# Two expert routers fed from the raw residual by halves, and expert weights requested before the routers run

## The reference, cut to what matters

```
h      = rmsnorm(x, g) * (1 + scale) + shift        # g, scale, shift: 1024 long
logits = h @ w_router + b_router                    # block 1: 32 experts, the 4 largest
                                                    # block 2: 4 groups + 4 x 8 experts: best group, 2 largest in it
w      = softmax of the chosen logits
x      = x + gate * sum over chosen experts of w * expert(h)
```

## Time and profile before

| | |
|---|---|
| median of 3 runs | 2306.01 us (2305.06 to 2310.74) |
| the profiled execution: its own time / its span | 2305.98 us / 2304.5 us |
| PE, DVE, ACT, POOL busy | 90%, 32%, 12%, 7% of the span |
| mean granted TensorE clock | 0.954 of full |
| read from memory | 645.92 MB, 281 GB/s over the span |
| stage mix1 ends, moe1's first expert product | 632.3 us, 667.8 us |
| moe1's last down product ends | 1603.4 us |
| mix2 ends, moe2's first expert product | 2002.9 us, 2055.0 us |

### The profile page before, as it was taken

The page is one execution under the profiler, slowest core; times in us unless marked ns, Lnnn a source line. Parts: engine busy times, 40 slices in busy tenths (PEclk is TensorE's granted clock), DMA queues, the critical chain, the costliest instruction groups (busy, mean ns, idle before and its releaser), DMA issues.

```text
span 2304.5 us, 22367 instructions
## 1 busy us (share of the span) xinstructions
PE 2070.7 (90%) x9445; PEld 1091.3 (47%) x9445; DVE 744.5 (32%) x1275; ACT 283.9 (12%) x633; POOL 156.6 (7%) x199
## 2 busy tenths in 40 slices
PE   3989999999879999999999999998989796879997
PEld 1644468755443333333333333332867595453332
DVE  2266858253231111111111111112354643332223
ACT  1111120121010000000000000000113021010000
POOL 3022420000000000000000000000200100000100
PEclk7999999999979999999999999999999896879999
DMA  7698710222298999999999999998422200359995
GB/s 282 236 381 330 276 48 22 100 74 74 84 409 356 428 427 428 427 427 428 427 427 428 427 427 427 428 427 346 145 81 102 73 1 5 123 241 422 420 421 219
DMA packets 91863, 648.55 MB, mean 281 GB/s; under 512 B 9952, under 2 KB 15256, under 8 KB 47440
## 3 DMA queue, kind: packets, MB, share of 16 engines
q1 hardware_dynamic: 87216, 640.41, 67.7%
q0 software_dynamic: 4544, 6.66, 1.0%
HBM read 645.92 MB, written 1.11 MB: 281 GB/s over the span
## 4 chain that ended last, share of the span: by engine, by line
PE 77%; DMA 13%; DVE 5%; ACT 2%; issue 2%; POOL 1%; SPq 0%; POOLq 0%; DVEq 0%; ACTq 0%
PE ps L218 35%; PE ps L1555 15%; DMA sb<-in_w_gate_up 7%; PE ps L1582 7%; PE ps L2367 5%; PE ps L1306 5%; DMA sb<-in_w_down 3%; PE ps L2391 2%; PE ps L223 2%; PE ps L1544 2%; PE ps L568 2%; DMA sb<-in_w_in 1%; PE ps L585 1%; DVE sb L920 1%; ACT sb L1299 1%
## 5 line engine op out<-in xcount | busy, mean ns | idle before, releaser
L218 PE MATMUL ps<-sb 128*128 128x128 f32 (+8 forms) x3878 | 867.3, 388 | 93.6 <-DVE sb L2312 13.7
L218 PEld LDWEIGHTS ps<-sb 128*128 128x128 f32 (+1 forms) x3878 | 612.7, 200 | 337.9 <-issue 233.8
L1555 PE MATMUL ps<-sb 128*64 128x512 f32 x2048 | 451.6, 597 | 2.9 <-DMA sb<-in_w_gate_up 2.1
L1555 PEld LDWEIGHTS ps<-sb 128*64 128x64 f32 x2048 | 143.8, 137 | 308.9 <-issue 289.5
L1582 PE MATMUL ps<-sb 128*64 128x512 f32 x1024 | 230.2, 604 | 51.4 <-DMA sb<-in_w_down 28.4
L1680 DVE TENSOR_SCALAR sb<-ps 128x512 f32<-128x512 f32 x32 | 33.6, 1049 | 497.9 <-PE ps L1555 497.9
L1582 PEld LDWEIGHTS ps<-sb 128*64 128x64 f32 x1024 | 86.1, 139 | 184.5 <-issue 184.5
L1317 DVE TENSOR_TENSOR sb<-ps,sb 128x512 f32<-128x512 f32 x64 | 44.3, 692 | 382.0 <-PE ps L1582 292.8
L223 PE MATMUL ps<-sb 128*128 128x128 f32 x455 | 79.2, 315 | 57.2 <-DVE sb L934 17.4
L2367 PE MATMUL ps<-sb 128*64 128x512 f32 x512 | 115.1, 603 | 4.5 <-POOL sb L2472 4.0
L1306 PE MATMUL ps<-sb 128*128 128x512 f32 x256 | 115.3, 593 | 1.7 <-DVE sb L1317 1.7
(11 more groups left out here) (331 smaller groups left out, 1056.0 us busy)
## 6 DMA issues: line engine op xcount, KB each, us to landing
sb<-in_w_gate_up SPq DMA_DIRECT2D x128, 2048.0 KB, 24.1
sb<-in_w_down SPq DMA_DIRECT2D x64, 2048.0 KB, 26.6
sb<-in_w_in SPq DMA_DIRECT2D x24, 2048.0 KB, 8.3
sb<-in_w1e SPq DMA_DIRECT2D x32, 1024.0 KB, 16.1
sb<-in_w3e SPq DMA_DIRECT2D x32, 1024.0 KB, 18.2
sb<-in_w2e SPq DMA_DIRECT2D x32, 1024.0 KB, 21.8
sb<-in_w_ada SPq DMA_DIRECT2D x24, 1024.0 KB, 9.0
sb<-in_w_mod SPq DMA_DIRECT2D x16, 1024.0 KB, 12.4
```

The costliest lines, as they stand in the source:

```text
L218: last = te.matmul(o, l, r, start=i == 0, stop=i == len(pairs) - 1)
L1555: last = te.matmul(ps[64 * h:64 * h + 64, 512 * c:512 * c + 512], xg[k][:, t, 64 * m:64 * m + 64], w[:, at:at + 512], start=False, stop=t ...
```

## The change

Both routers are computed from the raw `x`: the router weights are first multiplied by `G` in place, and `shift @ w` is added to the bias row. `G` and `shift` are brought into columns by one transpose (`mrt`), the constant is a product of 8 matmuls with a broadcast left side (`("cb", m)`). The output product runs with the token half outside, and the transposes of `x` and the logits are placed inside it and behind it, half by half. 1/rms is applied when the logits are read. The choice of experts is done for both halves in one instruction each, ranks are taken as soon as the mask stands, and the softmax comes after the ranks. `xn2` is written by ACT instead of DVE. Expert loads 0 to 6 wait for the end of attention (block 1) or for the recurrence's last product `("y", 1)` (block 2), and for the events at which the slots 2, 1 and 0 come free; the last weight loads of the mixers are issued between them.

```diff
@@ mix1: order of work
-        mix1 += [("gt", m, c, i) for m in range(2) for c in range(2) for i in range(2)]
-        mix1 += [("yT", t) for t in range(8)] + [("wo", c, i) for c in range(2) for i in range(2)]
+        mix1 += ["mrt"] + [("gt", 0, c, i) for c in range(2) for i in range(2)] + [("cb", 0)]
+        mix1 += [("gt", 1, c, i) for c in range(2) for i in range(2)]
+        mix1 += [("yT", t) for t in range(8)] + [("wo", 0, 0), ("wo", 1, 0), ("xt", 0, 0, 0), ("wo", 0, 1)]
+        mix1 += [("xt", 0, 0, 1), ("wo", 1, 1), ("lg", 0, 0), ("xt", 0, 1, 0), ("xt", 0, 1, 1), ("lg", 0, 1)]
@@ new helpers
+        def router_constant(m, wide):
+            o = opened(("cb", m))
+            mm(o[:, 0:wide], [(router[m][:, 0, f:f + 1].broadcast_to([128, 128]), wr[:, f, 0:wide]) for f in range(8)]) \
+                .then_inc(is_full(("cb", m)), 1)
+        def router_weights(m, wide):
+            o = filled(ve, ("cb", m))
+            ve.tensor_tensor(br[:, 0:wide], br[:, 0:wide], o[:, 0:wide], ADD).then_inc(dv.up(), 1)
+            ve.tensor_tensor(wr[:, :, 0:wide], wr[:, :, 0:wide], router[m][:, 1, :].unsqueeze(2).broadcast_to([128, 8, wide]), MUL) \
+                .then_inc(is_read(("cb", m)), 1)
+        def turn_x(m, i, c):
+            te.wait_ge(s["x_mix"], 4 * m + 2 * i + c + 1)
+            o = opened(("xt", m, i, c))
+            for k in range(4):
+                last = tr(o[:, 128 * k:128 * k + 128], x[:, i, 512 * c + 128 * k:512 * c + 128 * k + 128])
+            last.then_inc(is_full(("xt", m, i, c)), 1)
+        def logits(m, i, wide):
...
+                last = te.matmul(o[:, 0:wide], xT[:, f, 128 * i:128 * i + 128], wr[:, f, 0:wide], start=f == 0, stop=f == 7)
@@ tensor_mix1 (tensor_mix2 alike, with "wo2"; router_constant(1, 36) ahead of the "pa" products)
-            for c in range(2):
-                w = weights(next(order), r1)
-                for i in range(2):
+            w = [None, None]
+            for i in range(2):
+                for c in range(2):
+                    if i == 0:
+                        w[c] = weights(next(order), r1)
                     o = opened(("wo", c, i))
+                    mm(o, [(yT[:, t, 128 * i:128 * i + 128], w[c][:, t, :]) for t in range(8)]).then_inc(is_full(("wo", c, i)), 1)
+                    if (c, i) != (0, 0) and (c, i) != (1, 1):
+                        turn_x(0, 0, i)
+            logits(0, 0, 32)
+            turn_x(0, 1, 0)
+            turn_x(0, 1, 1)
+            logits(0, 1, 32)
@@ the choice
+        def top(k, src):
+            largest(src)
+            ve.tensor_tensor(chosen(k), iota..., idf..., ALU.is_equal).then_inc(dv.up(), 1)
+            settle()
+            ve.tensor_reduce(msk, chosen(k).rearrange("p i j e -> p i e j"), AX.X, ADD).then_inc(s["msk"], 1)
+            ve.tensor_scalar(rsm[:, :, 0:1], m8[:, :, 0:1], -1.0, None, MUL).then_inc(s["top"], 1)
+        def scalar_routed(m):
+            scalar_turned_x(m, 0, 0)
...
+            square(x[:, 0, :], stat[:, 0:1], 1024, 2048 * m)
+            scalar_turned_x(m, 0, 1)
+            scalar_turned_x(m, 1, 0)
...
+            square(x[:, 1, :], stat[:, 1:2], 1024, 2048 * m)
+            xn2_write(m)
+        def vector_logits(m, dst, wide):
+            for i in range(2):
+                if i:
+                    vector_turned_x(m, 1, 1)
+                o = filled(ve, ("lg", m, i))
+                ve.wait_ge(s["rstd"], 6 + 6 * m + i)
+                ve.scalar_tensor_tensor(dst[:, i, :], o[:, 0:wide], stat[:, 8 + i:9 + i], br[:, 0:wide], MUL, ADD) \
+                    .then_inc(is_read(("lg", m, i)), 1)
@@ tensor_moe1
-            tensor_turn(0)
-            te.wait_ge(s["wr"], 32)
...
             tensor_ranks(0)
+            gather(0)
+            te.wait_ge(s["msk"], 2)
             o = opened("cwT")
...
-            gather(0)
@@ loads
-            for n, upto in zip(range(2, len(r1.loads)), (5, 6, 9, 14, 16, 23, 30, 37, 44) + (48,) * 99):
+            for n, upto in zip(range(2, 20), (5, 6, 9, 14, 16, 23, 30, 37, 44) + (48,) * 99):
-        r2 = SlotTable(slots, rm.after())
+        r2 = SlotTable(slots, rm.after(), ids=(3, 4, 5, 6, 2, 1, 0))
         def sync_moe1():
-            sp.wait_ge(s["x_mix"], 4)
+            for n in range(4):
+                sp.wait_ge(*full_at(("av", 15)))
+                load(n, r2)
+                load(20 + n, r1)
+            sp.wait_ge(s["ymd"], 1)
+            load(4, r2)
+            sp.wait_ge(*full_at(("yT", 7)))
...
+            sp.wait_ge(*full_at(("wo", 0, 1)))
+            load(5, r2)
+            sp.wait_ge(*full_at(("wo", 1, 1)))
+            for n in range(6, len(r2.loads)):
                 load(n, r2)
         def sync_moe2():
-            sp.wait_ge(s["x_mix"], 8)
             for n in range(len(r4.loads)):
+                if n == 0:
+                    sp.wait_ge(*full_at(("y", 1)))
+                if n == 4:
+                    load(12, r3)
+                    sp.wait_ge(s["mT"], 8)
+                if n in (5, 6):
+                    sp.wait_ge(*full_at(("wo2", n - 5, 1)))
```

More of the change, by code:

```diff
@@ L1645, in scalar_moe1 @@
         def scalar_moe1():
-            ac.wait_ge(s["x_mix"], 4)
-            squares(x, stat[:, 0:16], 1024)
-            for i in range(2):
-                scalar_top(0, i, 4)
+            scalar_routed(0)
+            scalar_top(0, 4)
             scalar_gather(0, None)
@@ L1822, in sync_mix2 @@
         def sync_mix2():
-            for n in range(len(r3.loads)):
+            for n in range(12):
                 if n < 2:
@@ L1972, in tensor_mix2 @@
             te.wait_ge(s["mT"], 8)
-            for c in range(2):
-                w = weights(next(order), r3)
-                for i in range(2):
-                    o = opened(("wo2", c, i))
-                    mm(o, [(mT[:, j, 128 * i:128 * i + 128], w[:, j, :]) for j in range(8)]).then_inc(is_full(("wo2", c, i)), 1)
+            w = [None, None]
+            for i in range(2):
+                for c in range(2):
+                    if i == 0:
+                        w[c] = weights(next(order), r3)
+                    o = opened(("wo2", c, i))
+                    mm(o, [(mT[:, j, 128 * i:128 * i + 128], w[c][:, j, :]) for j in range(8)]).then_inc(is_full(("wo2", c, i)), 1)
+                    if (c, i) != (0, 0) and (c, i) != (1, 1):
+                        turn_x(1, 0, i)
+            logits(1, 0, 36)
+            turn_x(1, 1, 0)
+            turn_x(1, 1, 1)
+            logits(1, 1, 36)
         def scalar_gate(k):
@@ L2513, in vector_moe2 @@
+            settle()
+            ve.wait_ge(s["msk"], 4)
             for b in range(4):
```

292 lines of the change are left out of this document (151 added, 141 removed), and 3 rows, old and new, of the table row_src.

## The result

The changed kernel takes **2270.98 us**, the median of 4 runs (2270.72 to 2274.4); the kernel before takes 2305.54 (4 runs, 2305.06 to 2310.74). The ratio is 0.9848, 95% interval 0.9831 to 0.9866. 2275.5 was forecast, within 2266 to 2291. The profiled execution took 2271.23 us, its span 2269.7 against 2304.5: 34.8 us less, where 30.7 were forecast. The runs of the kernel before, here and beside the experiments, fall mostly into two groups, 2305 to 2308 and 2309 to 2313 us; why is open.

A forecast was written before the change was run, and what follows sets the result against it. Transfers through seven slots were taken to set the expert stages' end, which moves one for one with the first expert product. Gains of 14.5 (block 1) and 16.2 (block 2), 30.7 us off 2305.98, gave 2275.5 us, range 2266 to 2291.

The forecast's parts named there:

- The prefetch alone moves nothing: Expert stages: early loads only keep the seven slots full when the first expert product comes sooner; worth 0 alone.
- Without it a router shorter by 15 us would meet only four landed loads: Block 1: without early loads, a 15 us shorter router finds four loads landed instead of seven; no time given.
- The distance: Last output product to first expert product: block 1 from 36.9 to about 19 us, block 2 from 53.6 to about 36.
- Logits: Router, last output product to logits read: gain 11.1 us in block 1, 11.6 in block 2.
- E: The moment DVE starts on the last output product: 630.86 in block 1, 2001.45 in block 2, before the change.
- The choice: Router, logits read to ranks, both halves at once: gain 6.4 us in block 1, 5.3 in block 2.
- Ranks to the gather: Block 1's router: ranks the same 2.4 us, then 1.8 us to the gather becomes 0.7; gain 1.0.
- what moves E itself: Block 1, PE before the last output product: constant 1.9, `mrt` 0.2, eight transposes 1.3; 3.4 us lost.
- The clock section: Bounds outside the sum for ranks, gathers, logits and gated products at full or half clock; own range 2267 to 2288.
- The queue: Mixer loads between expert loads cost 0; as rival, delays of a whole load each return 24.5 us, 2300; chance 0.07.
- One stage that does not pass it on: Rival: transfers limit block 1 by themselves, so an earlier product finds the same end; 15 us less, 2291; chance 0.11.
- The lower clock in the experts: Rival: block 1's first gated products stay at 1.2 GHz, 13.95 us more each; four make 2331; chance 0.05.

The follow-up runs named there:

- e4_delay: The changed kernel with 7.2 us of unread DVE work ahead of block 1's choice of experts; 2280.34 us, ratio 0.9876.
- e2_early: The kernel before with the early expert loads alone and the buffers they need, routers as before; 2310.75 us, ratio 1.0007.
- e1_late: The changed kernel with the expert loads waiting for the whole finished x again, as before; 2281.18 us, ratio 0.9888.
- e3_choice: The kernel before with the choice for both halves at once and ranks ahead of the softmax, logits as before; 2299.75 us, ratio 0.9962.
- e10_after_again: The changed kernel run and traced once more, with nothing altered; 2270.69 us, ratio 0.9827.
- e7_fill: The changed kernel with products that nothing reads put in five of PE's pauses; 2266.24 us, ratio 0.981.
- e8_both: The changed kernel with block 1's router constant products and weight scaling moved into PE's pause, plus unread products in PE's pauses; 2260.7 us, ratio 0.9791.
- e9_more: e8_both with 20 more unread products in three pauses of mix2; 2264.05 us, ratio 0.9804.
- e11_both_again: e8_both run once more, on the same chip as e10_after_again; 2261.2 us, ratio 0.9792.
- e12_two: e9_more without the 8 unread products of the third gate; 2260.96 us, ratio 0.9794.
- e6_const: The changed kernel with block 1's router constant products and DVE's weight scaling moved into PE's 3.7 us pause before turning y; 2270.66 us, ratio 0.9832.

## Why the prediction was right, and where its terms were off

**What bounds the kernel.** Right: the end of block 1's experts moves with the first expert product (e4_delay), and loads that start sooner by themselves bring nothing (e2_early). "The prefetch alone moves nothing" holds, with a small cost not excluded. "Without it a router shorter by 15 us would meet only four landed loads" was the right warning without a price: it costs about 10 us of the gain (e1_late).

**Block 1.** The distance came to 18.1 us, 19.0 forecast. Logits: 11.9 gained, 11.1 forecast; they are read at E + 5.1. The forecast had the path over ACT and POOL as the later one, E + 5.7; in the trace 1/rms is ready at 641.56, E + 4.7, and DVE's wait ends with PE. The choice: 6.35 gained, 6.4 forecast; the comparison took 0.42 as taken, the reduction 0.60 instead of 0.42, and the rest 0.1 less. Both shares are counted as the prediction counts them. Their sum stands, but the border between them is drawn across the second half's logits: e3_choice puts the choice itself at 3.0. Ranks to the gather, ranks included: 1.6 gained, 1.0 forecast, since the ranks began at the full clock (1.66 us). From the gather to the first product 1.1 lost, 0.6 forecast: the gather took 6.26 instead of 5.34 us. `xn2` on ACT took 1.92 a half and was done at 644.4, 2.3 us ahead of the gather: nothing, as forecast.

**The term that was mis-sized** is "what moves E itself", 3.4. It measured 6.0: the constant and `mrt` 2.5, the transposes 0.9, and 2.6 that the first two output products took longer at the lower clock (16.58 against 14.00 us in e4_delay, at the same transfers). The net of block 1 was 12.8, not 14.5. The clock section had bounds for ranks, gathers, logits and gated products, and none for the output products, though the 2.9 that it had for a gated product is near in size. e10_after_again shows the 2.6 as a matter of the execution: there the term was 3.1, near the forecast's 3.4, and the net of block 1 15.7.

The Trainium skill (VectorE: DVE Perf Modes, The perf-mode tier table) lists both operations in fp32 at the same plain rate, which is what the prediction assumed of them without it. The two lines at 643 us speak against that for this layout: 256 elements in 0.42 and 0.60 us, the reduction reading with a stride along its inner axis. At 128 elements, in block 2, both took 0.29.

**Inside block 1's experts** nothing was forecast to change, and 1.65 us were gained: the third gated product took 13.95 us, 16.80 before. That too is the execution's: 15.39 in e10_after_again, where the whole stage took 939.0 us behind its first product, 3.3 more than before.

**Block 2.** The distance was 35.0, about 36 forecast. Logits 12.3 gained (11.6), the choice 5.1 (5.3), ranks to the gather 0.5 (0.6), the gather 0.6 (0). Between the start of mix2 and the last output product 0.9 lost, 1.3 forecast. Its parts are others than the forecast's: 1.0 for the transposes; 1.7 in the four products ahead of the constant's, which ran at 0.52 granted (3.5 us, 1.98 before) and held up DVE's chain to `pa`; 0.6 gained in the `pa` products; and 1.2 gained in the stretches ahead, where 2.4 lost in the 336 products is outweighed by others. The scaled weights cost nothing there, as forecast. At last 2.3 us came off the first gated product, which ran at the full clock; the clock section had priced it at 2.4 and left it out of the sum. Of the 4.1 us by which the change did better than forecast, 2.3 are these, 1.5 the distance and the output side of block 2, 2.0 the stage of block 1 and what lies right behind it, and 1.7 go off for block 1's net. Most of these are the clock's, and in e10_after_again the parts are others and the span is the same. So the mechanism is shown, and that the sum came within 4.1 us is in part luck: gains and losses at the clock that the sum left out cancelled in part.

**The queue.** 0, as forecast. `w_out_2`'s second half was not waited for: the output products of block 2 took 14.07 us for the first two and 7.03 for each of the others, with no wait for DMA among PE's. The four mixer loads in mix1 came in time as well; neither trace of the changed kernel has a wait of PE for them.

**The rivals.** One stage that does not pass it on: both did, within the clock's few us. The queue: no. The lower clock in the experts: the mechanism exists, with 2.2 us in one product (e4_delay) rather than 13.95 in each of four; the clock comes back within the product.

## What to carry to other kernels

Where a stage is paced by transfers through a few slots, write its end as the later of two sums: start of the stream plus the stream's length, first use plus the stage's length behind it. Here they are 960 and 934 us (up to 939 where products met the lower clock), and the 26 between them say roughly what a prefetch is worth (nothing at a distance of 35, about 10 at 16) and how much router can hide.

Count a step from the same event before and after. The batched choice looked like 6.4 us because it was counted from the first half's logits before and from both after; put in by itself it gave 3.0. The sum was right all the same, since what one share had too much the other had too little, and only a run of a part alone showed it.

A pause of PE on the path costs its own length and often the clock of the work behind it. Where it lies in a chain that another engine sets, faster products behind the pause only wait longer, as ahead of mix2's 336. Filling it is worth a try when the wait is known to the microsecond, and each filler must be found in the trace where it was meant to go.

## What the runs showed of the hardware

TensorE's clock was at 1.2 GHz (0.50 granted) behind the pause ahead of `y`'s turning (3.7 us), in the gather behind block 1's ranks (their pause 2.5) and in block 2's ranks (pause 4.3: 2.34 us, 1.30 in e7_fill), at 0.57 on the mean in the first 4 us of `pa` (12), and at 2.4 again within the dense products that follow; in the first trace of the changed kernel it rose at about 610, the output products having begun at 605.61. A pause is not the whole of it: in e7_fill and e8_both block 1's gather ran at 0.72 on the mean though the pause ahead of the ranks was filled, and at the full clock (3.84 us) in e9_more, e11_both_again and e12_two with the same fillers. The largest loss in one product is 2.9 us. Which of the stretches are hit differs between executions of one program, as the two traces of the changed kernel show. The runs of one kernel lie up to 8 us apart (e6_const), those of the kernel before up to 10 (2301.67 to 2312.03).

The Trainium skill (TensorE: Matmul & The Clock Gate, Part 1: The HAM clock gate) puts it as a gate that stands at half by default and that activity opens, and says that the same kernel finds it in another phase from run to run. The traces agree with both: e7_fill's fillers bring `pa` from 15.68 to 14.08 us, and the first output products of the changed kernel took 16.58 and 14.00. The same page holds the ramp to be under 1% of a kernel and not worth fitting; the times here are under 1% too, but e7_fill took off 4.7 us, 0.2%, and e8_both, fillers and the moved constant together, 9.5 to 10.3, 0.4%, nearly a third of what the whole change brought.

ACT's `xn2`, 1024 elements written with a stride, took 1.92 us a half, where a square of the same size takes 1.03 and DVE took 1.2 for the same half.

What stays open: whether a kernel can be arranged so that none of its stretches meets the lower clock. e12_two gained 2.7 us at one place and no time in all, and why other stretches were hit wasn't separated. Open too are the two groups of the kernel before, and whether early loads with the long router cost a few us (e2_early).
